# Attention step of a fused decoder kernel: scores and values side by side, nine projection products in two portions

## What is computed

```python
q = (x @ w_q).reshape(..., N_HEADS, 2, HEAD_DIM)      # HEAD_DIM 64
k, v = shared_kv(x, kv_norm, w_kv)
s = einsum('bqhcd,bkhcd->bhcqk', q, k) * ATTN_SCALE + bias
p = softmax(s)
w = p[:, :, 0] - lam * p[:, :, 1]
out = einsum('bhqk,bkhe->bqhe', w, v)
o = rmsnorm(out, subln) * (1.0 - lam_init)
y = o.reshape(...) @ w_o
```

## Time and profile before

| | us |
|---|---|
| median of 3 runs | 2745.07 |
| the profiled execution | 2744.36 |
| its span, first to last instruction | 2742.5 |
| TensorE busy in the span | 2620.1 (96%) |
| VectorE busy | 1435.1 (52%) |
| ScalarE busy | 687.3 (25%) |
| GpSimd busy | 839.6 (31%) |
| mean granted TensorE clock | 0.983 |

### The profile page before, as it was taken

How to read it: one execution, slowest core, us unless ns; L and a number is a source line. 1 busy time by engine, 2 the same in 40 slices (tenths; PEclk the granted TensorE clock), 3 DMA queues, 4 the chain that set the end, 5 groups by cost and what they waited for, 6 DMA issues and landing times.

```text
span 2742.5 us, 40115 instructions
## 1 busy us (share of the span) xinstructions
PE 2620.1 (96%) x16836; PEld 2546.9 (93%) x16836; DVE 1435.1 (52%) x2237; ACT 687.3 (25%) x1143; POOL 839.6 (31%) x464
## 2 busy tenths in 40 slices
PE   5999999999999999989999999799999999999995
PEld 4999999999999999988999998699999999999995
DVE  6666355444444444484555555436545544444446
ACT  4445131111111111132444445412111111111111
POOL 2342323322333332243343332032333223333221
PEclk8999999999999999999999999899999999999998
DMA  3111311111111111114233333211111111111111
GB/s 133 35 43 39 110 47 44 42 47 47 47 47 47 44 42 47 47 63 168 86 97 94 95 101 121 100 47 46 47 43 43 47 47 47 47 40 46 47 47 70
DMA packets 79329, 171.09 MB, mean 62 GB/s; under 512 B 9477, under 2 KB 44805, under 8 KB 78894
## 3 DMA queue, kind: packets, MB, share of 16 engines
q1 hardware_dynamic: 72098, 140.57, 16.2%
q10 hardware_dynamic: 7052, 27.96, 2.7%
HBM read 146.46 MB, written 26.76 MB: 63 GB/s over the span
## 4 chain that ended last, share of the span: by engine, by line
PE 87%; DVE 7%; ACT 3%; issue 2%; POOL 1%; ACTq 0%; DVEq 0%; POOLq 0%
PE psum L709 70%; PE psum L851 3%; PE psum L855 3%; PE psum L853 3%; PE psum L904 2%; PE psum L880 2%; DVE line L1475 2%; DVE x L1540 2%; PE psum L892 1%; ACT line L1226 1%; DVE line L1516 1%; POOL w_lo L610 1%; DVE inverse_rms L1528 0%; PE psum L963 0%; DVE line L1496 0%
## 5 line engine op out<-in xcount | busy, mean ns | idle before, releaser
L709 PE MATMUL psum<-xn_hi,w_hi 128*128 128x352 f32 x3120 | 680.4, 326 | 32.9 <-DVE xn_lo L1522 13.8
L709 PE MATMUL psum<-xn_lo,w_hi 128*128 128x352 f32 x3120 | 675.1, 324 | 0.0
L709 PE MATMUL psum<-xn_hi,w_lo 128*128 128x352 f32 x3120 | 674.6, 324 | 0.0
L606 POOL TENSOR_SCALAR w_hi<-w_raw 128x1024 fp32r<-128x1024 f32 x176 | 190.4, 1082 | 1514.5 <-PE psum L709 1499.6
L709 PEld LDWEIGHTS psum<-xn_hi,w_hi 128*128 128x128 f32 x3120 | 534.7, 190 | 36.4 <-issue 21.9
L709 PEld LDWEIGHTS psum<-xn_lo,w_hi 128*128 128x128 f32 x3120 | 538.0, 189 | 0.0
L709 PEld LDWEIGHTS psum<-xn_hi,w_lo 128*128 128x128 f32 x3120 | 532.8, 189 | 0.0
L610 POOL TENSOR_TENSOR w_lo<-w_raw,w_hi 128x1024 fp32r<-128x1024 f32 x176 | 454.6, 2583 | 14.7
L1226 ACT ACTIVATE line<-line,columns 128x1072 f32<-128x1072 f32 x96 | 123.4, 1285 | 1063.3 <-DVE line L1498 1063.3
L1540 DVE TENSOR_TENSOR x<-psum,x 128x1056 f32<-128x1056 f32 x208 | 261.1, 1256 | 228.7 <-PE psum L709 227.9
L1493 DVE TENSOR_TENSOR line<-psum,inverse_rms 128x704 f32<-128x704 f32 x104 | 92.8, 893 | 473.6 <-PE psum L709 473.5
(11 more groups left out here) (214 smaller groups left out, 2530.8 us busy)
## 6 DMA issues: line engine op xcount, KB each, us to landing
w_raw<-in_w SPq DMA_DIRECT2D x200, 512.0 KB, 3.4
k_pages<-in_cache_k SPq DMA_DIRECT2D x128, 64.0 KB, 2.1
v_pages<-in_cache_v SPq DMA_DIRECT2D x128, 64.0 KB, 2.0
scratch_line<-scratch_row ACTq DMA_DIRECT2D x1, 4608.0 KB, 19.3
x<-in_x ACTq DMA_DIRECT2D x8, 528.0 KB, 10.8
scratch_x<-x ACTq DMA_DIRECT2D x1, 4224.0 KB, 13.6
out_k<-raw ACTq DMA_DIRECT2D x8, 528.0 KB, 2.7
out_v<-raw ACTq DMA_DIRECT2D x8, 528.0 KB, 3.2
```

Source lines behind the costliest of these rows:

```text
L606: pool.tensor_scalar(WHI[:, s], WRAW[:, s], 1.0, 0.0, ALU.mult, ALU.add).then_inc(w_hi, 1)
L709: last = pe.matmul(PS[:, 3 * (a % 2) + c, 0:CH], w[:, s, k, :], r[:, c * CH:(c + 1) * CH], start=start and first, stop=stop and final)
```

## The change

The order of work inside an attention step changes on TensorE and on VectorE; ScalarE, GpSimd and the queues keep theirs. On TensorE `values(g-3)` moves from behind the second portion to directly behind `scores(g)`. The nine products come in portions of 5 and 4 (`PART` is 5) instead of 3, 3 and 3: five before `turn_weights(g-2)` and four behind the sample's part. `turn_values` and the sample's parts therefore follow `turn_weights` with no products between. In `ring_order` the event "o" of a step moves ahead of the step's "w" events (for steps after the loop it stays). On VectorE the copy `output_rows` moves from the start of step g + 4 to behind `biased` of step g + 3, and the two calls of `evac_chunks` take what is complete at the step's start and after its first five products.

```diff
 RATE = 9
+PART = 5
@@ ring_order
         h, t = divmod(g, 8)
+        if 3 <= g < STEPS:
+            order.append(("o", g - 3))
         if 2 <= g < STEPS + 2:
             order += [("w", g - 2, b) for b in range(halves(g - 2))]
...
-        if g >= 3:
+        if g >= STEPS:
             order.append(("o", g - 3))
@@ TensorE's loop
                 scores(g)
-                fill(RATE // 3)
+                if g >= 3:
+                    values(g - 3)
+                fill(PART)
                 if g >= 2:
                     turn_weights(g - 2)
                 if t == 2:
                     turn_values(h)
-                fill(RATE // 3)
                 if t == 0:
                     sample_scores(h)
...
                 if t == 5:
                     sample_turn(h)
-                if g >= 3:
-                    values(g - 3)
-                fill(RATE - 2 * (RATE // 3))
+                fill(RATE - PART)
                 if h and t >= 6:
                     turn_output(h - 1, t - 6)
@@ VectorE's loop
                 h, t = divmod(g, 8)
-                if g >= 4:
-                    output_rows(g - 4)
...
                 biased(g)
-                evac_chunks(chunks_by(g, RATE // 3))
+                if g >= 3:
+                    output_rows(g - 3)
+                evac_chunks(chunks_by(g, 0))
                 if g:
                     combine(g - 1)
...
-                evac_chunks(chunks_by(g, 2 * (RATE // 3)))
+                evac_chunks(chunks_by(g, PART))
                 if g >= STEPS - 6:
                     low_o(g - (STEPS - 6))
-            output_rows(STEPS - 4)
             combine(STEPS - 1)
             output_rows(STEPS - 3)
```

## The result

The changed kernel takes 2754.2 us (median of 8 runs, 2751.82 to 2758.86), the kernel before 2744.73 (8 runs, 2743.81 to 2745.24) in the same comparison: a ratio of 1.0038, 95% interval 1.0027 to 1.0048. It is slower by 9.5 us. The forecast was 2753.6 in a range from 2747 to 2761.

The account below looks back on a forecast made before the run. TensorE's list alone was taken to bound the kernel up to step 56, a VectorE-ScalarE circle the tail. Seven heads at 1.02 us (7.1) plus tail 1.4 gave +8.5 us: 2753.6 us for the median, range 2747 to 2761.

Parts of the forecast that it names:

- Rival A: The forecast itself: two ring waits a head and a slightly longer tail, +8.5 us; chance 60%.
- The waits at t = 5 and t = 2: TensorE waits for ScalarE's read of turned weights, 0.66 us a head, and of turned values, 0.57 us a head.
- "Scores to values": Extra time when values directly follow scores on TensorE: 0.10 us a step taken, possibly 0 or 0.21; no row showed it.
- Rival B: Values behind scores cost 0.05 or less, or reads come sooner: 2746 to 2750 us (+5.8, +4.2 or +1.4); chance 23%.
- rival C: Faster: values behind scores free (-5.8), ScalarE's reads not waited for, copies out of the circle (-1.2): 2738 us; chance 5%.
- The covers at t = 3: Five products hide half 1's wait for VectorE's copy with 0.3 us left; chunks finished in the second portion have as little.
- rival E: Much slower: t = 3 cover fails by 0.3 to 0.6 a head, tail gives nothing back: +14 to +16, 2760; chance 10%.
- rival D: Each of 14 new waits brings a stretch of lowered TensorE clock, 1.7 us lost each: +24, 2777; chance 2%.
- The tail: Last steps without products: +4.75 us by the end of step 63, 3.4 less behind `high_o`, net +1.4.
- the circle: Sets the tail's end: VectorE's passes over the scores, ScalarE's exponentials and `high_o`, VectorE's `low_o`; +4.75 us by step 63's end.

Follow-up runs that it names:

- portions of 5, 2, 2: Changed kernel with two of the last four products put ahead of the sample's part at t = 2 and t = 5: 2746.13 us, ratio 1.0007 to the kernel before.
- copy first: Changed kernel with VectorE's copy of the values result ahead of its passes over the scores in steps 57 to 63: 2749.59 us, ratio 1.0021 to the kernel before.
- tail with early copy: Kernel before in steps 0 to 56; changed order in steps 57 to 63 with the values copy ahead of the passes: 2743.46 us, ratio 0.9996.
- cover and copy: Changed kernel with portions 5, 2, 2 at t = 2 and 5, and the values copy ahead of the passes in steps 57 to 63: 2744.07 us, ratio 0.9994.
- both undone: Changed kernel with portions 5, 2, 2 at t = 2 and 5, and the order of before in steps 57 to 63: 2743.14 us, ratio 0.9999.
- the steady state alone: Changed order in steps 0 to 56 only, steps 57 to 63 as in the kernel before: 2753.59 us, ratio 1.0031 to the kernel before.
- the changed kernel again: The changed kernel repeated without edits, on the chip of three other variants: 2754.19 us, ratio 1.0038 to the kernel before.
- all three repairs: Changed kernel with portions 5, 2, 2 at t = 2 and 5, 5, 4, 0 in step 2, and the values copy early in steps 57 to 63: 2741.65 us.
- The portions alone: Kernel before with its old values place, ring and copy, but products in portions of 5 and 4: 2771.89 us, ratio 1.0101 to the kernel before.
- the tail alone: Kernel before in steps 0 to 56 with portions 3, 3, 3; changed order in steps 57 to 63: 2747.81 us, ratio 1.0013.

## Why the prediction was right, and where it was not

**Rival A held**: two ring waits a head and a longer tail. 9.5 us were measured, 8.5 forecast. That the total came so near is in part luck: both terms were too small in the profile (7.1 for 8.1, and 1.4 for 3.7), and their errors don't show in full in the median.

**The waits at t = 5 and t = 2** cost 0.76 and 0.66 us (1.44 - 0.68; 0.70 - 0.04) for forecasts of 0.66 and 0.57. Each is 0.1 larger for one reason. I let TensorE move on 0.05 after ScalarE's read ends, as it does within the turned values, but 0.14 to 0.15 passes here (1623.01 + 0.60 to 1623.75; 1599.73 to 1599.88). Together with smaller terms a head grew by 1.16 instead of 1.02 (head 0 is another matter: there the sample's probabilities do come late, see below). The portions of 5, 2, 2 show the cause: the head goes back to 62.0.

**"Scores to values"** was in no row and was taken as 0.10. That is what it is: 6, 8, 10 and 14 values go from 0.59, 0.81, 1.04 and 1.47 us to 0.69, 0.91, 1.14 and 1.59 from their start to the next work, while 12 and 16, which already stood behind the sample's matmuls, don't change. Rival B (0.05 or less) and rival C (nothing) fall by this. (Rival B's last figure is also wrong in itself: 8.5 less seven times 1.23 is -0.1, not +1.4.) With 0.11 saved, the point of two portions, fewer changes of shape, is nearly all paid back.

**The covers at t = 3** held. In front of half 1 there is no wait up to step 56, so the steady state's half of rival E falls. Its other half, a tail that gives little back, is what came.

**The clock** (rival D): the two new waits in each head left it at 1.00 in the steady windows, and the +24 us didn't come. The Trainium skill's page TensorE: Matmul & The Clock Gate, section "A second HAM failure mode: psum-queue depth-cycling", says that frequent short idles between groups of matmuls can make the clock swing. The trace doesn't bear that out for two waits of 0.4 to 0.5 us in each 63 us: the windows of 10 us from 1300 to 1700 all show 1.00.

**The tail** is the step that failed. The hand count of the circle was near: exponentials of steps 57, 59, 61 and 63 start 1.90, 4.29, 4.88 and 5.41 us later after head 7's first scores, for 1.95, some 3.6, 4.0 and 4.75. But I gave 3.4 us back, because "these turned weights and values of step 61 run while ScalarE and VectorE are still in the circle". Only the turned weights do. "o" of step 61 stands in the ring two places behind the second half of head 6's turned output, which ScalarE reads behind the last `high_o`. So values wait for `o_t_head`, 2.48 us on their line, and then run 2.87 us. From the end of `high_o` of step 63 to the projection it was 10.2 us and is 8.5 (1760.77 to 1769.27): 1.7 come back, and 5.4 - 1.7 = 3.7 is the tail's excess in the profile. I had checked the ring for the event that moved, and not for the event that I wanted to run early. The place of the copy is the main cause of the 5.4, but not cleanly measured: with it ahead of the passes 4.6, 4.8 and 2.5 us come off in three pairs of kernels, and what is left in the circle depends on the clock. `o_t_head` of the last step starts 56.31 us after head 7's first scores in the changed kernel and 50.90 before; with the early copy it is 50.34 where the clock held (copy first), and 52.60 and 53.37 where it did not (tail with early copy, cover and copy). So the early copy gives a tail level with the old one, not a better one. The 5.4 too holds time at a lowered clock: 0.50 from 1728 to 1732, at step 59's transposes.

**The two errors and the median.** 8.1 for seven heads and 3.7 for the tail would be 11.8, over the measured 9.5. The profile of an execution near the median is not there, so where 2 us of this go stays open. These 2 us are within what equal orders show: the last stretch took 61.65 with both undone and 63.26 with the steady state alone, and from step 56 on these two kernels issue the same instructions. The clock moves with such differences: the four slowest of the changed kernel's 8 runs have a mean granted clock of 0.981, the four fastest 0.982.

## What to carry to other kernels

Where events share two banks in a fixed order, removing work between two of them makes a wait out of a read that nobody had to think about. For each event, ask what stood between it and the one two places before, and how long that one's read takes. Cheap filler work belongs exactly there, and two products in each of two places were worth 7.6 us here (6.2 and 10.2 in two other pairs of kernels). Where a list has no filler, put the short copy that frees a bank ahead of the long passes; 0.28 us of work gave 2.5 to 4.8 here. It then ties the passes to the work that fills the bank, and to that engine's clock. Before you count on something running early, look up which event must be read before it may start.

## What the runs showed of the hardware that was not expected

In the first head the sample's probabilities come late, because VectorE's last pass over them takes five times as long as in later heads (2.26 us at 1279.86, against 0.43 at 1598.04). It runs beside a pass of GpSimd that makes the low parts of weights, and ends 0.17 us after it. The changed kernel:

```profile
1278.76 3.19 POOL L675 TENSOR_TENSOR w_lo<-w_raw,w_hi 128x1024 fp32r<-128x1024 f32 x1
1279.86 2.26 DVE L1922 TENSOR_SCALAR sample_probs<-sample_probs,sample_stats,sample_row_factor 128x288 f32<-128x288 f32 x1
```

Ten of the 13 profiles have this overlap, with VectorE's pass at 2.25 to 2.28 us and GpSimd's at 3.18 to 3.21. In the three others GpSimd was done 1.4 us before VectorE began, and they took 0.43 and 2.37 to 2.40. TensorE, which now comes to them with five products ahead of it in the step instead of six, waits 3.61 us instead of 2.63: counted from the first scores it arrives 0.5 us earlier, and VectorE is ready 0.5 later. The line of the changed kernel, and its windows of 4 us from there:

```profile
1282.17 0.40 PE L949 MATMUL psum<-ident,sample_probs 128*32 128x128 f32 x1 [3.61 <-DVE sample_probs L1922]
```

```profile
1280.00:1284.00 4.00, 1.83 (x8) 1.83 (x9) 2.55 (x5) 0.34 (x3) 1.94 (x1) 0.54 0.21 39
1284.00:1288.00 4.00, 4.00 (x21) 3.36 (x20) 0.00 (x0) 0.00 (x0) 0.00 (x0) 0.60 0.74 235
1288.00:1292.00 4.00, 4.00 (x31) 3.79 (x28) 3.56 (x10) 0.45 (x1) 0.84 (x1) 1.00 0.48 126
```

The same of the kernel before:

```profile
1281.34 0.28 PE L946 MATMUL psum<-ident,sample_probs 128*32 128x128 f32 x1 [2.63 <-DVE sample_probs L1920]
```

```profile
1280.00:1284.00 4.00, 2.66 (x19) 2.32 (x21) 2.15 (x6) 0.34 (x3) 1.12 (x1) 1.00 0.42 132
1284.00:1288.00 4.00, 4.00 (x32) 3.72 (x29) 2.94 (x9) 1.20 (x3) 0.00 (x0) 1.00 0.59 161
```

After 2.63 us of idle time the granted clock stayed at 1.00; after 3.61 us two windows show 0.54 and 0.60, which lie between the levels of 1.2 and 2.4 GHz, nearer the lower. 21 matmuls instead of 32 fit into the second. The head is 3.9 us longer in this profile, of which some 0.5 is VectorE being ready later and some 0.8 the new ring wait at t = 5; the rest goes with the lowered clock. In the other profiled executions idle times of 3.37, 3.28 and 3.13 us before this matmul (the copy first, the changed kernel again, the steady state alone) come with a lowered clock too, and heads of 64.5 to 64.7. Those of 2.71 us and less come with a clock of 1.00 and heads of 58.1 to 61.6, with one exception: all three repairs have 1.78 us there, 0.91 and 0.66 in the two windows, and 61.5. So the length of this one wait is not all that decides, and no run here isolates it. Three of the four long heads stand in the slowest run of their kernel. Moving the four products ahead of the place took the excess out of the profile and not out of the median, so in most executions it is probably absent. Nor is the wait fixed by the order. The portions alone, whose step 2 has the changed kernel's order up to this wait, waits 1.09 us there; the tail alone, with the steady order of before, 0.65; cover and copy not at all. These are the three profiles in which GpSimd was done before VectorE's pass. It had been waiting for its weights from the DMA (8.22 us in the tail alone, 9.83 in the kernel before, whose order in this head is the same), so when they arrive decides whether the two passes meet. What decides that, and what sets the clock in the one exception, is open.
